# Attention without normalised probabilities: scaling the results by turned inverse sums

## What is computed

```python
sc = (jnp.einsum('bqhd,bkhd->bhqk', qn, k_nope)
      + jnp.einsum('bqhr,bkr->bhqk', qr, k_rope))
p = jax.nn.softmax(sc.astype(jnp.float32) * scale, axis=-1).astype(v.dtype)
return jnp.einsum('bhqk,bkhd->bqhd', p, v)
```

## Time and profile before

| | us |
|---|---|
| median of 3 runs | 2642.54 (2639.04 to 2643.63) |
| the profiled execution | 2641.86 |
| its span, first to last instruction | 2640.1 |
| TensorE busy over the span | 2347.7 (89%) |
| VectorE busy | 1130.1 (43%) |
| ScalarE busy | 659.1 (25%) |
| GpSimd busy | 308.3 (12%) |

### The profile page before, as it was taken

One profiled execution on the slowest core, in us unless ns is written; L12 is line 12 of the kernel. 1 busy time (PEld: TensorE's weight loads), 2 busy tenths in 40 slices (PEclk: granted clock), 3 DMA queues, 4 the chain that ended last, 5 costly groups with the idle time before them and its releaser, 6 DMA issues. The chain is left out here.

```text
span 2640.1 us, 26908 instructions
## 1 busy us (share of the span) xinstructions
PE 2347.7 (89%) x10834; PEld 1945.3 (74%) x10834; DVE 1130.1 (43%) x1461; ACT 659.1 (25%) x884; POOL 308.3 (12%) x145
## 2 busy tenths in 40 slices
PE   6999999999978896895957877699799999999997
PEld 5888888888867876785846666577688888888885
DVE  4333333333244394586345666551433333333325
ACT  4211111111022321414225565421321111111112
POOL 1000000000000011110007777500100000000000
PEclk8999999999988998897978999899899999999998
DMA  3211111111021322221330000051221111111101
GB/s 127 80 48 48 46 43 46 48 48 48 16 76 47 89 72 37 64 88 32 120 89 5 6 6 1 31 217 40 64 80 47 44 46 48 48 48 48 48 24 64
DMA packets 174038, 146.95 MB, mean 56 GB/s; under 512 B 27968, under 2 KB 154176, under 8 KB 173952
## 3 DMA queue, kind: packets, MB, share of 16 engines
q1 hardware_dynamic: 173952, 145.77, 18.4%
HBM read 120.58 MB, written 23.07 MB: 54 GB/s over the span
## 5 line engine op out<-in xcount | busy, mean ns | idle before, releaser
L48 PE MATMUL psum<-f_nT_hi,f_w_hi 128*128 128x512 f32 x1408 | 551.6, 392 | 23.9 <-DVE rows L584 23.9
L49 PE MATMUL psum<-f_nT_lo,f_w_hi 128*128 128x512 f32 x1408 | 549.0, 390 | 0.0
L50 PE MATMUL psum<-f_nT_hi,f_w_lo 128*128 128x512 f32 x1408 | 548.4, 390 | 0.0
L48 PEld LDWEIGHTS psum<-f_nT_hi,f_w_hi 128*128 128x128 f32 x1408 | 264.9, 188 | 86.1 <-DVE rows L584 27.8
L584 DVE SCALAR_TENSOR_TENSOR rows<-psum,rows 128x1024 f32<-128x1024 f32 x176 | 215.4, 1224 | 221.2 <-PE psum L50 221.2
L50 PEld LDWEIGHTS psum<-f_nT_hi,f_w_lo 128*128 128x128 f32 x1408 | 264.7, 188 | 55.5
L49 PEld LDWEIGHTS psum<-f_nT_lo,f_w_hi 128*128 128x128 f32 x1408 | 264.9, 188 | 54.3
L48 PE MATMUL psum<-f_d_hi,f_hT_hi 128*128 128x512 f32 x704 | 275.3, 391 | 7.3 <-issue 7.3
L49 PE MATMUL psum<-f_d_lo,f_hT_hi 128*128 128x512 f32 x704 | 275.2, 391 | 0.0
L50 PE MATMUL psum<-f_d_hi,f_hT_lo 128*128 128x512 f32 x704 | 275.1, 391 | 0.0
L532 DVE TENSOR_TENSOR f_w_lo<-f_raw,f_w_hi 128x1024 fp32r<-128x1024 f32 x80 | 97.7, 1221 | 398.2 <-ACT f_w_hi L528 398.2
(11 more groups left out here) (278 smaller groups left out, 3410.1 us busy)
## 6 DMA issues: line engine op xcount, KB each, us to landing
f_raw<-ffn_w_gate SPq DMA_DIRECT2D x44, 512.0 KB, 4.8
f_raw<-ffn_w_up SPq DMA_DIRECT2D x44, 512.0 KB, 3.8
f_raw<-ffn_w_down SPq DMA_DIRECT2D x44, 512.0 KB, 3.5
g_raw<-w_in SPq DMA_DIRECT2D x16, 512.0 KB, 4.6
gates<-rows SPq DMA_DIRECT2D x10, 512.0 KB, 3.0
rows<-x SPq DMA_DIRECT2D x8, 512.0 KB, 7.9
kept<-rows SPq DMA_DIRECT2D x1, 4096.0 KB, 12.8
gl_gate<-gates SPq DMA_DIRECT2D x8, 512.0 KB, 4.8
```

The costliest lines, as they stand in the source:

```text
L48: pe.matmul(out, lhs_hi, rhs_hi, start=first, stop=False)
L49: pe.matmul(out, lhs_hi, rhs_lo, start=False, stop=False)
L50: return pe.matmul(out, lhs_lo, rhs_hi, start=False, stop=last)
```

## The change

The exponentials are turned and multiplied with V as they are. The 128 row sums of a tile are kept for four tiles at a time (`tot` is [P, 2, 4]). VectorE takes the reciprocal of them once for each group J of four tiles, spread over 64 columns ([128, 4, 64], 256 elements in a row). TensorE turns that into bank 7 (`inverses(J)`, 4 transposes), so that each query's inverse sum stands in a column over the 64 rows of the head's output. VectorE then adds the two halves of the output (`total`) and multiplies with the turned inverses out of bank 7 (`att`). GpSimd's pass over the exponentials is gone.

With it the lag goes from 3 to 2, `prob` has three slots of its own (`SLOTS_P`), the jobs of the projection and the queries stand one tile earlier, and the order inside a step changes on every engine. Since bank 7 now also holds the turned inverses, a job for the queries' first half or for the keys' first half of head 2 and later waits until they are read (`av`). `PARTS` is 1, so that a turned tile is read out whole, as before; the code has a second form for 2. `att` moves to another place in memory.

```diff
-        KD, HALF_R, LAG = NOPE + ROPE, ROPE // 2, 3
-        PROJECT_AT, QUERIES_AT = (1, 2, 5, 6), (3, 4)
+        KD, HALF_R, LAG, SLOTS_P, PARTS = NOPE + ROPE, ROPE // 2, 2, 3, 1
+        PROJECT_AT, QUERIES_AT = (0, 1, 4, 5), (2, 3)
...
+        tot = sb("tot", [P, 2, 4])
+        inv = sb("inv", [P, 2, 4, VH])
...
# tensor, project(n, x)
                 elif n:
                     pe.wait_ge(s["proj_act"], job)
                     pe.wait_ge(s["proj_dve"], job)
+                    if n >= 2 and x in (0, 2):
+                        pe.wait_ge(s["av"], 2 * n - 3 + x // 2)
...
+            def inverses(J):
+
+                pe.wait_ge(s["inv"], J + 1)
+                pe.wait_ge(s["proj_act"], min(2 * JOBS + 2 * J, HEADS * JOBS))
+                pe.wait_ge(s["proj_dve"], min(2 * JOBS + 2 * J, HEADS * JOBS))
+                for i in range(4):
+                    t = pe.transpose(inv_out[:, i * P:(i + 1) * P], inv[:, J % 2, i, :], ident[:])
+                t.then_inc(s["inv_t"], 1)
...
# tensor, the loop
             for g in range(G + LAG + 2):
+                turning = LAG <= g < G + LAG
+                if turning:
+                    turn(g - LAG, 0)
                 if g < G:
                     scores(g)
-                if LAG <= g < G + LAG:
-                    turn(g - LAG)
...
                 if values_after(g):
                     values(*values_after(g))
+                    if values_after(g)[1] == 1:
+                        inverses(values_after(g)[0])
                 if g < G and job_after(g):
                     project(*job_after(g))
...
# scalar, the loop
+                if 1 <= g <= G:
+                    exponential(g - 1)
+                if LAG <= g < G + LAG:
+                    turned(g - LAG, 0)
                 if g and values_after(g - 1) and values_after(g - 1)[1] == 1:
                     spread_out(values_after(g - 1)[0])
-                if g and g - 1 < G and job_after(g - 1):
-                    project(*job_after(g - 1))
...
+                if g < G and job_after(g):
+                    project(*job_after(g))
                 if h + 1 < HEADS and qt in QUERIES_AT:
                     queries(h + 1, QUERIES_AT.index(qt))
-                if LAG <= g < G + LAG:
-                    turned(g - LAG)
-                if g < G:
-                    exponential(g)
                 if g and values_after(g - 1) and values_after(g - 1)[1] == 1:
                     attended(values_after(g - 1)[0])
...
# vector
+            def inverse(J):
+
+                dve.wait_ge(s["exp"], 4 * J + 4)
+                if J >= 2:
+                    dve.wait_ge(s["inv_t"], J - 1)
+                dve.reciprocal(inv[:, J % 2], tot[:, J % 2].unsqueeze(2).broadcast_to([P, 4, VH])).then_inc(s["inv"], 1)
...
                 dve.wait_ge(s["spread"], J + 1)
+                dve.tensor_tensor(total[:], pv_out[0:VH], spread[:], ALU.add).then_inc(s["sum"], 1)
+                dve.wait_ge(s["inv_t"], J + 1)
                 if J >= 2:
                     dve.wait_ge(s["av_lo"], J - 1)
-                dve.tensor_tensor(att[rows, J % 2, :], pv_out[0:VH], spread[:], ALU.add).then_inc(s["av"], 1)
+                dve.wait_ge(s["sum"], J + 1)
+                dve.tensor_tensor(att[rows, J % 2, :], inv_out, total[:], ALU.mult).then_inc(s["av"], 1)
...
# vector, the loop
-                if 1 <= g <= G:
-                    inverse(g - 1)
+                if g >= 5 and g % 4 == 1 and g // 4 - 1 < NB:
+                    inverse(g // 4 - 1)
+                if LAG <= g < G + LAG:
+                    turned(g - LAG, 0)
+                if g < G:
+                    maximum(g)
...
                 if g and values_after(g - 1) and values_after(g - 1)[1] == 1:
                     attended(values_after(g - 1)[0])
-                if g and g - 1 < G and job_after(g - 1):
-                    project(*job_after(g - 1))
-                if g < G:
-                    maximum(g)
-                if LAG <= g < G + LAG:
-                    turned(g - LAG)
+                if g < G and job_after(g):
+                    project(*job_after(g))
...
# gpsimd
-            def normalized(g):
-                sl = g % LAG
-                pool.wait_ge(s["inv"], g + 1)
-                pool.tensor_scalar(prob[:, sl, :], prob[:, sl, :], inv[:, sl:sl + 1], None, ALU.mult).then_inc(s["norm"], 1)
```

More of the change, by code:

```diff
@@ L1422, in attention_phase @@
         rot = sb("rot", [P, 2, HALF])
-        prob = sb("prob", [P, LAG, SEQ])
+        prob = sb("prob", [P, SLOTS_P, SEQ])
         PT_lo = sb("PT_lo", [P, 3, ST, 2 * P], F32R)
-        nmx, tot, inv = (sb(n, [P, LAG]) for n in ("nmx", "tot", "inv"))
-        spread = sb("spread", [VH, HALF])
-        att = sb("att", [P, 2, HALF])
+        nmx = sb("nmx", [P, SLOTS_P])
+        tot = sb("tot", [P, 2, 4])
+        inv = sb("inv", [P, 2, 4, VH])
+        spread, total = sb("spread", [VH, HALF]), sb("total", [VH, HALF])
+        att = at("att", [P, 2, HALF], F32, 24 * KB)
         names = ("trig wv_in wv_hi wv_lo lt l_hi l_lo rot0 kr kr_hi kr_lo v_mm v_hi v_lo raw_in w_hi w_lo proj proj_act proj_dve rot q_sum q_hi q_lo "
-                 "scores nmx exp inv norm tr tr_hi tr_lo pv spread av av_hi av_lo").split()
+                 "scores nmx exp inv inv_t tr tr_hi tr_lo pv spread sum av av_hi av_lo").split()
         s = {n: sem(n) for n in names}
@@ L1443, in attention_phase @@
         job_bank = lambda n, x: psum[:, x if n == 0 else 7, :]
+        inv_out = psum[0:VH, 7, :]
         wq = lambda a, k: a[:, k * P:(k + 1) * P]
@@ L1529, in scores, with turn @@
                 mm.then_inc(s["scores"], 1)
-            def turn(g):
-                pe.wait_ge(s["norm"], g + 1)
+            def turn(g, x):
+                if x == 0:
+                    pe.wait_ge(s["exp"], g + 1)
                 if g == 0:
@@ L1535, in turn @@
                 else:
-                    pe.wait_ge(s["tr_lo"], g)
-                for k in range(ST):
-                    t = pe.transpose(turned_bank[:, k, :], prob[:, g % LAG, tile(k)], ident[:])
+                    pe.wait_ge(s["tr_lo"], (g - 1) * PARTS + x + 1)
+                for k in range(KP):
+                    t = pe.transpose(turned_bank(x)[:, k, :], prob[:, g % SLOTS_P, tile(x * KP + k)], ident[:])
                 t.then_inc(s["tr"], 1)
+            def inverses(J):
[5 more added lines that the diff above has]
+                t.then_inc(s["inv_t"], 1)
             def values(J, part):
                 if part == 0:
-                    pe.wait_ge(s["tr_lo"], 4 * J + 4)
+                    pe.wait_ge(s["tr_lo"], (4 * J + 4) * PARTS)
                     if J:
-                        pe.wait_ge(s["av"], J)
+                        pe.wait_ge(s["sum"], J)
                 for k in range(4 * part, 4 * part + 4):
@@ L1615, in spread_out @@
                 if J:
-                    act.wait_ge(s["av"], J)
+                    act.wait_ge(s["sum"], J)
                 act.copy(spread[:], pv_out[VH:2 * VH]).then_inc(s["spread"], 1)
@@ L1743, in _, with queries @@
         def _(pool):
[L1744 to L1749, removed]
+            def queries(n, x):
+                if n * 2 + x:
+                    pool.wait_ge(s["q_lo"], n * 2 + x)
+                if n and x == 0:
+                    pool.wait_ge(s["av_lo"], attended_by(n))
                 pool.wait_ge(s["rot"], n * 2 + x + 1)
@@ L1754, in queries, with attended_by, attended @@
                 pool.tensor_tensor(QT_lo[0:KD, n % 2, hs(x)], qf[0:KD, x, :], QT_hi[0:KD, n % 2, hs(x)].bitcast(F32), ALU.subtract).then_inc(s["q_lo"], 1)
-            def normalized(g):
-                sl = g % LAG
-                pool.wait_ge(s["inv"], g + 1)
-                pool.tensor_scalar(prob[:, sl, :], prob[:, sl, :], inv[:, sl:sl + 1], None, ALU.mult).then_inc(s["norm"], 1)
-            def attended(J, normed, asked):
+            def attended_by(n):
+                at = (n - 1) * ST + QUERIES_AT[0]
+                return sum(1 for g in range(at) if values_after(g) and values_after(g)[1] == 1)
+            def attended(J, asked):
                 h = J // 2
                 rows = slice(h % 2 * VH, (h % 2 + 1) * VH)
-                if h % 2:
-                    pool.wait_ge(s["norm"], normed)
-                    pool.wait_ge(s["q_lo"], asked)
+                pool.wait_ge(s["q_lo"], asked)
+                if J:
+                    pool.wait_ge(s["av_lo"], J)
                 pool.wait_ge(s["av_hi"], J + 1)
@@ L1771, in _ @@
             for x in range(2):
-                queries(0, x, 0)
+                queries(0, x)
             for g in range(G + LAG + 3):
                 h, qt = g // ST, g % ST
[L1775 to L1779, removed]
                 if h + 1 < HEADS and qt in QUERIES_AT:
-                    queries(h + 1, QUERIES_AT.index(qt), g)
+                    queries(h + 1, QUERIES_AT.index(qt))
                     asked += 1
```

(2 more changed lines are left out.)

47 lines of the change are left out of this document (25 added, 22 removed).

## The result

| | us |
|---|---|
| before, median of 4 runs | 2640.89 (2639.04 to 2643.63) |
| after, median of 4 runs | 2694.01 (2693.57 to 2694.82) |
| ratio after to before | 1.020, 95% interval 1.0184 to 1.0216 |
| span of the profiled execution, before and after | 2640.1 and 2693.0 |

The change costs 53 us, 2.0%. The forecast was slower, at 2690 us.

A forecast was written before the change was run, and what follows sets the result against it. It took a chain of hand-overs to bound the kernel before, with ScalarE waiting 60.3 us for GpSimd. Loop +53.2 and tail -5.0 gave net +48.2 on 2641.9: 2690 us, range 2668 to 2708.

The forecast's parts named there:

- The ring of a plain step: In steps without a group's output read: maximum, exponential, cast and subtraction in series on VectorE and ScalarE, 4.55 us.
- The held steps: Every fourth step, reading a group's output: exponential and jobs wait for `att`; 10.54 us (queries), 8.63 (keys), 6.35 (no job).
- The reciprocal: VectorE's new reciprocal of 256 elements: taken at 1.8 us, between 0.4 and 3.6; hidden behind a keys' job.
- the rival with the reciprocal at its upper end: The reciprocal takes 3.6 us and delays held steps further: +25, 2715 us; 7 in 100.
- The start: Tiles 0 to 2: first job ahead of `scores(1)` and the first exponential, about 9.5 us against 7.03, +2.5.
- The tail: From the last maximum to the end of `aT_lo`: 18.6 us against 23.6, -5.0.
- The sum: The loop from first to last maximum, all steps added: 351.1 us against 297.9, +53.2.
- The clock held: Rival: TensorE keeps its full clock in the held jobs, together 12 us less: 2678 us; 10 in 100.
- The ring without holds: Rival: exponentials and jobs not held by `att`, 61 steps of 4.55 us: 2626 us; 6 in 100.
- TensorE as the bound: Rival: the loop shrinks to TensorE's busy time, steps of about 4.0 us: 2591 us; 4 in 100.

The follow-up runs named there:

- e6: e5 with ScalarE casting the output one step later and the reciprocal over 4 elements in a row instead of 256; 2630.8 us, ratio 0.9952.
- e1: The changed kernel with VectorE's maximum ahead of the subtraction for the turned tile instead of behind it; 2731.6 us, ratio 1.0325.
- e2: The changed kernel without turned inverses, maximum ahead of subtraction, scores ahead of turning, output cast one step later; 2626.7 us, ratio 0.9929.
- e5: The changed kernel without turned inverses, output multiplied by itself, so jobs do not wait for the read output; 2660.8 us, ratio 1.0067.
- e7: The changed kernel with 17 unused matmuls on TensorE in each of 12 stands ahead of a waiting job; 2680.0 us, ratio 1.0149.
- e8: The changed kernel with the reciprocal over the 4 sums alone, transposes reading each inverse 64 times; 2689.3 us, ratio 1.0175.
- e9: e4 with the reciprocal and transposes of e8; 2605.3 us, ratio 0.9857.
- e3: The kernel before with GpSimd's normalising pass left out and nothing in its place, results not scaled; 2601.5 us, ratio 0.9834.
- e4: The changed kernel's complete arithmetic in the queue order, lag and job places of the kernel before; 2619.2 us, ratio 0.9902.

## Why the prediction was right, point by point

- **The ring of a plain step** was forecast at 4.55 us and is 4.53, within 0.04 in 42 of the 47 steps of that kind. e6 shows the ring alone, e1 and e2 that it follows the order.
- **The held steps**: forecast 10.54 (queries), 8.63 (keys), 6.35 (no job); measured 10.72 to 10.76, 8.53 to 8.84 and 6.58. Each piece is in the rows above: the job starts 2.77 us behind the maximum (2.66), takes 2.90 (2.92), the exponential starts at 6.70 (6.62). The job starts late because `att` begins 0.14 us behind the end of `total`, where 0.03 was taken. TensorE stood 4.62 us, where some 4.2 were taken, and the clock was as forecast. e5 and e7 show that the jobs' wait and the clock are parts of it, by 35 and 14 us, which overlap, since a job that does not wait does not lose the clock.
- **The reciprocal** was in no row and was taken at 1.8 between 0.4 and 3.6 us; it is 1.74, 6.2 ns for each element beyond the first, near the slope of the narrow ones. So the rival with the reciprocal at its upper end (3.6 us, 2715) falls. The estimate worked out from the Trainium skill (VectorE: DVE Perf Modes, First, the fixed hardware budget), 2.3 us, was too long, as the rows had it. e8 shows that it was on the path in the queries' steps and hidden behind the keys' jobs.
- **The start** took 9.50 us from tile 0 to tile 2, forecast 9.5. **The tail** is 1760.59 - 1741.90 = 18.7 us, forecast 18.6.
- **The sum**: forecast 351.1 us from the first maximum to the last, measured 1741.90 - 1387.45 = 354.5. Of the 3.4 missing, 1.6 are the held steps with jobs, 0.5 the two without, and 2.2 are five plain steps that took 4.77 to 5.49; the other 42, each 0.02 shorter than forecast, give 0.9 back. Four of the five are in the last head. There no job follows, so TensorE's stand was not costed. But it stands there too, and eight transposes then take 1.94 us instead of 1.07. The row of TensorE, and the same place in e7 and e8, whose last heads have the same work for TensorE:

```profile
1732.31 1.94 PE L1545 MATMUL psum<-ident,at_prob 128*128 128x128 f32 x8 [4.12 <-DVE at_PT_lo L1718]
...
1714.88 1.38 PE L1549 MATMUL psum<-ident,at_prob 128*128 128x128 f32 x8 [4.12 <-DVE at_PT_lo L1722]
...
1725.27 1.53 PE L1545 MATMUL psum<-ident,at_prob 128*128 128x128 f32 x8 [4.13 <-DVE at_PT_lo L1718]
```

The steps that begin there took 4.77, 4.53 and 4.52 us. Counting the two such places of the last head in the changed kernel, e5, e7 and e8, the three with transposes of 1.94 us have steps of 4.77 and behind them 4.95 to 5.49; the five with 1.12 to 1.64 us have 4.52 or 4.53 and behind them 4.68 or 4.69. So it is the clock that lengthens them, as far as traces side by side can show it.

- **Not forecast**: the loop itself began 1.9 us later than before (1387.45 against 1385.53). The loops of the nine experiments began between 1382.4 (e7, with the change in it) and 1388.9 (e1), so this belongs to the spread of the phases ahead, not to the change.
- **The rivals.** The clock held (2678): it did not by itself, and e7, which held it by force, gives 2680. The ring without holds (2626): e6 made it, 2631. TensorE as the bound (2591): only with ring and holds both gone and the reciprocal small, e9, 2605, and e3, 2601; this rival's price was 10 to 15 us too hopeful, since it let TensorE never stand. In the prediction's terms the gain of GpSimd's pass is real, 43 us (e3). By the ratios, what ate it up is the jobs' wait for the read output with its lower clock (35 us, e5), the rest of the holds with the wide reciprocal (30, from e5 to e6), and what still parts e6 from e3, the ring and VectorE's new product (31).

## What to carry to other kernels

When work is taken off an engine and the code's order is changed with it, write down for each engine what stands ahead of what in one step, and follow the releases around: a closed loop that passes each engine once per step sets the step, whatever the busy shares say, and its length can be added up from start-to-start times in the trace of before. Look at each instruction that waits for something which stands behind its own releaser, and ask what else is queued behind that wait. The waits for a shared bank were 1 us each in one order (e4) and 4.6 us in the other, where they cost 35 us; test the new arithmetic in the old order first.

## What the runs showed of the hardware

- A reciprocal of 128x256 took 1.74 us on VectorE, 6.2 ns for each further element, five times the 1.2 ns of a subtraction or maximum of 1024; over 4 elements 0.16 us. TensorE turned a column read 64 times by a step of zero in the same 272 ns per transpose as a stored copy.
- After a stand of 4.62 us TensorE was granted 0.50 of its clock, the 1.2 GHz level, from its first matmul at 1520.34 until about 1525.1, over the job, eight transposes and the first matmul of the scores. Filling the stand with matmuls of no use won 14 us (e7). The length of the stand alone does not tell the level: in e1 eight transposes behind a stand of 1.84 us took 1.64 us at 1519.76 and 1.07 us at 1623.03.
